# A two-block transformer kernel: the gated linear recurrence reordered, with its decay from an exponential

## The reference

```python
def rg_lru(x, gate_a_w, gate_a_b, gate_x_w, gate_x_b, a_param):
    ...
    r = jax.nn.sigmoid(block_diag(gate_a_w, gate_a_b))
    i = jax.nn.sigmoid(block_diag(gate_x_w, gate_x_b))
    log_a = -LRU_C * r * jax.nn.softplus(-a_param.astype(jnp.float32))
    a = jnp.exp(log_a)
    u = jnp.sqrt(-jnp.expm1(2.0 * log_a)) * (i * x.astype(jnp.float32))
    _, h = lax.associative_scan(linear_combine, (a, u), axis=1)
    return h.astype(x.dtype)

def recurrent_mixer(x, w_in, conv_w, conv_b, gate_a_w, gate_a_b, gate_x_w, gate_x_b, a_param, w_out):
    gate, xr = jnp.split(x @ w_in.astype(x.dtype), [LRU_WIDTH], axis=-1)
    xr = causal_depthwise_conv(xr, conv_w, conv_b)
    h = rg_lru(xr, gate_a_w, gate_a_b, gate_x_w, gate_x_b, a_param)
    return (h * jax.nn.gelu(gate)) @ w_out.astype(x.dtype)
```

## Time and profile before

| what | value |
|---|---|
| time, median of 3 runs | 2933.91 us (2926.31 to 2934.51) |
| the profiled execution's own time | 2934.61 us |
| its span, first to last instruction | 2932.8 us |
| mean granted clock of PE | 0.982 of full speed |
| busy share of the span | PE 96%, DVE 46%, ACT 42%, POOL 42% |
| moved by DMA | 259.21 MB, mean 88 GB/s |
| slabs of weights | 470 in all, 26 made while the recurrence runs |

### The profile page before, as it was taken

One profiled execution on the slowest core, in us unless ns is written; L12 is line 12 of the kernel. 1 busy time (PEld: TensorE's weight loads), 2 busy tenths in 40 slices (PEclk: granted clock), 3 DMA queues, 4 the chain that ended last, 5 costly groups with the idle time before them and its releaser, 6 DMA issues.

```text
span 2932.8 us, 32425 instructions
## 1 busy us (share of the span) xinstructions
PE 2823.6 (96%) x12948; PEld 2281.5 (78%) x12948; DVE 1341.9 (46%) x2091; ACT 1223.7 (42%) x1793; POOL 1236.8 (42%) x550
## 2 busy tenths in 40 slices
PE   8998999999889999998999999999989999999998
PEld 7786788888667888876778788888767777888886
DVE  4565651545875415435656452022246565531113
ACT  3564442434544424334574434233235744342231
POOL 4222344444453444432446444444423464444442
PEclk9999999999989999998999999999999999999999
DMA  4211232232212323322222223232322222223232
GB/s 146 82 59 61 79 101 97 92 107 87 79 65 94 99 91 98 101 92 74 66 65 94 86 94 101 94 100 94 101 72 66 72 79 87 100 94 101 94 101 72
DMA packets 73926, 259.21 MB, mean 88 GB/s; under 512 B 9184, under 2 KB 9184, under 8 KB 73776
## 3 DMA queue, kind: packets, MB, share of 16 engines
q1 hardware_dynamic: 71680, 251.79, 26.8%
q10 hardware_dynamic: 2096, 5.36, 0.5%
HBM read 254.95 MB, written 2.13 MB: 88 GB/s over the span
## 4 chain that ended last, share of the span: by engine, by line
PE 85%; DVE 8%; ACT 3%; issue 2%; POOL 1%; DMA 0%; DVEq 0%; SPq 0%; ACTq 0%; POOLq 0%
PE ps L420 25%; PE ps L422 25%; PE ps L421 25%; PE ps L486 2%; PE ps L516 1%; PE ps L541 1%; PE ps L542 1%; PE ps L543 1%; POOL w_lo L1859 1%; PE ps L499 1%; PE ps L431 1%; PE ps L468 1%; PE ps L470 1%; PE ps L469 1%; ACT w_hi L872 1%
## 5 line engine op out<-in xcount | busy, mean ns | idle before, releaser
L1859 POOL TENSOR_TENSOR w_lo<-raw,w_hi 128x1024 fp32r<-128x1024 f32 x470 | 1135.6, 2419 | 1552.0 <-ACT w_hi L872 1551.6
L420 PE MATMUL ps<-xs,w_hi 128*128 128x512 f32 x2176 | 864.2, 397 | 17.8 <-POOL w_lo L1859 10.3
L421 PE MATMUL ps<-xs,w_hi 128*128 128x512 f32 x2176 | 849.3, 390 | 0.0
L422 PE MATMUL ps<-xs,w_lo 128*128 128x512 f32 x2176 | 849.0, 390 | 0.0
L872 ACT ACTIVATE w_hi<-raw 128x1024 fp32r<-128x1024 f32 x470 | 493.9, 1052 | 660.4 <-PE ps L422 615.4
L420 PE MATMUL ps<-hid,w_hi 128*128 128x512 f32 x1320 | 523.0, 396 | 43.7 <-DVE att L1736 18.1
L421 PE MATMUL ps<-hid,w_hi 128*128 128x512 f32 x1320 | 519.2, 393 | 0.0
L422 PE MATMUL ps<-hid,w_lo 128*128 128x512 f32 x1320 | 519.1, 393 | 0.0
L420 PEld LDWEIGHTS ps<-xs,w_hi 128*128 128x128 f32 x2176 | 409.7, 188 | 123.9 <-issue 15.0
L421 PEld LDWEIGHTS ps<-xs,w_hi 128*128 128x128 f32 x2176 | 410.0, 188 | 88.3 <-issue 4.8
L422 PEld LDWEIGHTS ps<-xs,w_lo 128*128 128x128 f32 x2176 | 409.8, 188 | 86.3
(11 more groups left out here) (212 smaller groups left out, 2651.8 us busy)
## 6 DMA issues: line engine op xcount, KB each, us to landing
raw<-in_weights SPq DMA_DIRECT2D x470, 512.0 KB, 3.5
hT<-in_x ACTq DMA_DIRECT2D x4, 512.0 KB, 9.6
btab<-in_rel SPq DMA_DIRECT2D x8, 256.0 KB, 3.7
out<-tmp ACTq DMA_DIRECT2D x8, 256.0 KB, 2.0
btab<-in_heads SPq DMA_DIRECT2D x6, 256.0 KB, 3.7
tmp<-in_heads SPq DMA_DIRECT2D x6, 256.0 KB, 4.4
common<-in_fixed ACTq DMA_DIRECT2D x1, 642.0 KB, 13.3
small<-in_small ACTq DMA_DIRECT2D x1, 368.5 KB, 5.0
```

Of the source, the lines that this page charges most:

```text
L420: pe.matmul(banks[bank][:], wh, rh, start=(k == 0), stop=False)
L421: pe.matmul(banks[bank][:], wh, rl, start=False, stop=False)
L422: last = pe.matmul(banks[bank][:], wl, rh, start=False, stop=(k == len(specs) - 1))
L1859: gp.tensor_tensor(w_lo[:, n % NPAIR, :], raw[:, n % NRAW, :], w_hi[:, n % NPAIR, :].bitcast(F32), ALU.subtract).then_inc(*w_low.tick(n))
```

## The change

It touches `rec_early` and the stage of the recurrence in each engine's program. The decay a is now an exponential on ACT (L1116 of the changed kernel) of the first tanh; 1-a is then made on DVE as (a+1) times the tangent, and a as one minus that, so the reciprocal goes. The tangent is written to PSUM bank 6 or 7 and the second sigmoid's tanh in place in bank 5, both by ACT, and DVE reads them there. ACT does the exponentials of two tiles and then their square roots together, at c = 3, 5, 7 and 9 (`rec_2`). DVE scans tile c-3, ahead of the taps of tile c, and multiplies the gated input of tile c-1 last. On POOL the product for tile c-3 stands behind the slabs. The banks of `rec_out` are taken in order, its early parts begin at c = 8, and tiles 6 and 7 both are left for the end.

```diff
-        rec_banks = (0, 1, 2, 3, 6, 7, 4, 5)
-        rec_early = {7: [(o, 0, 3) for o in (0, 1, 4, 5)],
-                     8: [(o, 3, 4) for o in (0, 1, 4, 5)] + [(2, 0, 4), (3, 0, 4)],
-                     9: [(o, 4, 6) for o in range(6)], 10: [(o, 6, 7) for o in range(6)]}
+        rec_early = {8: [(o, 0, 4) for o in range(4)], 9: [(4, 0, 4), (5, 0, 4)], 10: [(o, 4, 6) for o in range(6)]}
...
-                    free[bank] = (act, (name, c))
+                free[4], free[5] = (act, ("rec_a", c)), (vec, ("rec_g", c))
...
+            for c in (6, 7):
+                free[c] = (vec, ("rec_w", c))
             for o in range(8):
-                rec_out(o, 7 if o < 6 else 0, 8)
-                free[rec_banks[o]] = (resid, ("rec", o))
+                rec_out(o, 6 if o < 6 else 0, 8)
+                free[o] = (resid, ("rec", o))
...
-                ac.activation(r, r, ACT.Tanh, bias=sp8[:, c:c + 1], scale=sp8[:, c:c + 1]).then_inc(*act.tick(("rec_t", c)))
-                A.wait_ge(act, ("rec_t", c))
-                ac.activation(u, r, ACT.Sqrt).then_inc(*act.tick(("rec_u", c)))
+                if c >= 2:
+                    A.wait_ge(vec, ("rec_w", c - 2))
+                ac.activation(banks[6 + c % 2][:], e, ACT.Tanh, bias=sp8[:, c:c + 1], scale=sp8[:, c:c + 1]).then_inc(
+                    *act.tick(("rec_t", c)))
+
+            def rec_2(tiles):
+
+                for c in tiles:
+                    e = ring(c)[0]
+                    A.wait_ge(act, ("rec_t", c))
+                    ac.activation(e, e, ACT.Exp, bias=s1[:, c:c + 1], scale=s1[:, c:c + 1]).then_inc(*act.tick(("rec_e", c)))
+                for c in tiles:
+                    ac.activation(ring(c)[1], banks[6 + c % 2][:], ACT.Sqrt, scale=0.25).then_inc(*act.tick(("rec_u", c)))
...
             for c in range(12):
+                if c < 8:
+                    weights(("rec_g", c))
+                if c == 0:
+                    root(2)
+                if c in (3, 5, 7, 9):
+                    rec_2((c - 3, c - 2))
                 if 0 <= c - 4 < 8:
                     rec_4(c - 4)
...
-            def rec_2(c):
-                r, gi, u = ring(c)
-                xc, q = att[:, 8 + c, :], tmp[:, 4 + c % 4, :]
-                V.wait_ge(act, ("rec_t", c))
-                if c >= 4:
-                    V.wait_ge(pool, ("rec_y", c - 4))
-                chain(ve.tensor_scalar(q, r, -1.0, -1.0, ALU.mult, ALU.add))
+            def rec_1(c):
                 V.wait_ge(act, ("rec_i", c))
-                ve.scalar_tensor_tensor(out=gi, in0=gi, scalar=1.0, in1=xc, op0=ALU.add, op1=ALU.mult)
+                V.wait_ge(taps, ("rec", c))
+                ve.scalar_tensor_tensor(out=ring(c)[2], in0=banks[5][:], scalar=1.0, in1=att[:, 8 + c, :], op0=ALU.add,
+                                        op1=ALU.mult).then_inc(*vec.tick(("rec_g", c)))
+
+            def rec_3(c):
+
+
+                e, u, gi = ring(c)
+                xc = att[:, 8 + c, :]
+                V.wait_ge(act, ("rec_u", c))
+                chain(ve.scalar_tensor_tensor(out=u, in0=e, scalar=1.0, in1=u, op0=ALU.add, op1=ALU.mult))
+                ve.scalar_tensor_tensor(out=e, in0=e, scalar=1.0, in1=banks[6 + c % 2][:], op0=ALU.add, op1=ALU.mult).then_inc(
+                    *vec.tick(("rec_w", c)))
                 V.wait_ge(step)
-                chain(ve.reciprocal(q, q))
+                V.wait_ge(vec, ("rec_g", c))
+                chain(ve.tensor_tensor(gi, gi, u, ALU.mult))
+                V.wait_ge(vec, ("rec_w", c))
+                chain(ve.tensor_scalar(e, e, -1.0, 1.0, ALU.mult, ALU.add))
                 V.wait_ge(step)
...
+                ve.tensor_tensor_scan(xc, e, gi, 0.0, ALU.mult, ALU.add).then_inc(*vec.tick(("rec_scan", c)))
```

More of the change, by code:

```diff
@@ L1077, in scalar, with rec_gate, rec_in, rec_high @@
             network(0, 1)
[L1080 to L1085 removed]
+            def rec_gate(c):
                 A.wait_ge(scaled, ("rec_g", c))
[L1087 removed]
+                ac.activation(att[:, c, :], banks[2 * (c % 2)][:], ACT.Gelu_apprx_tanh).then_inc(*act.tick(("rec_g", c)))
+            def rec_in(c):
                 A.wait_ge(scaled, ("rec_x", c))
[L1089 removed]
+                ac.activation(att[:, 8 + c, :], banks[2 * (c % 2) + 1][:], ACT.Identity, bias=col("rec_conv_b", c),
                               scale=col("rec_conv_w", 4 * c + 3)).then_inc(*act.tick(("rec_x", c)))
+            def rec_high(c):
                 A.wait_ge(taps, ("rec", c))
@@ L1120, in scalar @@
                 if c < 8:
-                    rec_0(c)
+                    weights(("rec_x", c))
+                    rec_gate(c)
+                if 0 <= c - 1 < 8:
+                    weights(("rec_a", c - 1))
+                    weights(("rec_i", c - 1))
+                if c < 8:
+                    rec_in(c)
                 if 0 <= c - 1 < 8:
                     rec_1(c - 1)
+                if c < 8:
+                    rec_high(c)
                 for o, k0, k1 in rec_early.get(c, ()):
@@ L1563, in rec_0 @@
             def rec_0(c):
-                bg, bx = 2 * (c % 2), 2 * (c % 2) + 1
+                bx = 2 * (c % 2) + 1
                 xc, ps = att[:, 8 + c, :], banks[bx]
-                if c == 0:
-                    root(2)
-                scale(bg, ("rec_g", c), 2, ("rec_g", c))
                 scale(bx, ("rec_x", c), 2, ("rec_x", c))
@@ L1611, in vector @@
             for c in range(12):
+                if c == 0:
+                    root(2)
+                if c < 8:
+                    scale(2 * (c % 2), ("rec_g", c), 2, ("rec_g", c))
                 if 0 <= c - 3 < 8:
                     rec_3(c - 3)
-                if 0 <= c - 2 < 8:
-                    rec_2(c - 2)
                 if c < 8:
                     rec_0(c)
+                if 0 <= c - 1 < 8:
+                    rec_1(c - 1)
             for o in range(8):
-                residual(rec_banks[o], o, ("rec", o), 3, ("rec_out", o))
+                residual(o, o, ("rec", o), 3, ("rec_out", o))
```

45 lines of the change are left out of this document (13 added, 32 removed).

## The result

The changed kernel takes **2925.4 us** (median of 16 runs, 2921.5 to 2928.4) against 2934.1 us (16 runs, 2926.0 to 2935.4) of the kernel before on the same chip. The ratio is 0.9975, 95% interval 0.9967 to 0.9983: some 7.3 us saved (the medians are 8.7 us apart). The sign of the forecast and its range hold; the size does not, since 17.2 us were forecast.

A forecast was written before the change was run, and what follows sets the result against it. The recurrence's loop between DVE and ACT was taken as the bound, PE idling for it. The last operand coming 17.2 us earlier, with the end costing nothing, gave 2934.6 - 17.2 = 2917 us; range 2903 to 2932.

The forecast's parts named there:

- What bounds: In the recurrence, the loop between DVE and ACT sets the pace at 15.26 us per tile, and PE idles for it.
- a floor of 62.0 us for five passes: Recurrence, c = 3 to 7 without meetings with POOL: three odd and two even passes, 41.7 + 20.3 us.
- DVE's wait for the roots at odd c: Sign of being right: in the loop DVE waits 2 to 3 us for ACT's square root at odd c, at even c not.
- I take the middle, 2.6: Recurrence: DVE's meetings with POOL cost 2.6 us per tile, between 2.1 and 3.1; over five passes 13 us.
- then POOL, ACT, POOL 1.26 + 0.63 + 1.26: End of the recurrence: last three terms of the DVE route to the last operand, 26.4 us in all plus 5.2 of meetings.
- costs nothing as long as that chain covers it: Last stretch: PE's 105 matmuls instead of 90, 23.8 + 2.4 us, stay under the 27.3 us chain of DVE and ACT.
- The high part of tile 7 ends near 811 us: Sign of being right: ACT's high part of tile 7 ends at 810.7 us, before at 820.7.
- a last stretch over 27.3: Sign of being wrong: last operand to next root exceeds 27.3 us because PE's 105 matmuls, not the residual chain, fill it.
- Rival (b): Gain eaten, no change: meetings of 3.7 us or more per tile make the end's DVE route count; 2931 us, chance 0.17.
- rival (a): PE becomes the bound: meetings with POOL nearly vanish in the loop, 29.3 us saved, 2905 us; chance 0.17.
- (c): Slower: POOL's every instruction is met in the recurrence, 7 us per tile, 2949 us; chance 0.08.
- (d): Change does not do what it says: ACT or DVE far slower on PSUM in place, loop as before, 2934 us; chance 0.03.

The follow-up runs named there:

- e2: Changed kernel with POOL making only 32 of 1024 columns of each slab's low part in the recurrence; stage 153.9 us against the changed kernel's 177.0.
- e4: Changed kernel with POOL's product of tile c-3 moved behind the gate's slab, ahead of the low part and the input's slab; stage 163.5 us, ratio 0.9941.
- e6: Changed kernel with POOL's late slabs of c = 10 issued with those of c = 11, behind tile 7's low part; stage 172.6 us, ratio 0.9952.
- e11: Changed kernel with tile 6's product made early at c = 11, one tile left for the end; stage 174.2 us, ratio 0.9964.
- e10: Kernel before with only the new table of the early output product and banks in plain order; stage 178.7 us, ratio 0.9978.
- e5: Changed kernel with POOL's whole order from the kernel before: low part, product, then slabs; stage 174.5 us, ratio 0.9966.
- e9: Kernel before with only POOL's order altered: gate's slab, product, low part, input's slab; stage 184.4 us, ratio 1.0000.
- e3: Changed kernel with 1-a written in place in PSUM, so the TENSOR_SCALAR reads PSUM; stage 172.9 us, ratio 0.9961.
- e8: Changed kernel with exponential and root made for one tile in every pass instead of batches of two; stage 175.8 us, ratio 0.9960.

## Why the prediction was right in sign and wrong in size

- **What bounds** was right: the loop between DVE and ACT, until tile 7, and then the way to the last operand. So was the recurrence's own path: a floor of 62.0 us for five passes against 64.5 in e2; table loads at 1.28 us; PSUM operands never met, at 0.68 us instead of the 0.75 assumed; DVE's wait for the roots at odd c, 2.8, 3.8 and 3.8 us instead of 2 to 3.
- **The first failed step is "I take the middle, 2.6".** The five passes, from 731.78 to 811.05, took 79.3 us, so (79.3 - 62.0) / 5 = 3.5 us per tile in place of 2.6: 4.3 of the 4.5 us missing in the loop. (It is what the passes take above the path without meetings; the four groups by themselves lose 3.0 us per tile, as a mean of all eight.) Even the upper bound of 3.1 was too low. It took the meetings as a rate that goes with the number of exposed instructions. They go with the place: the changed kernel's run of five begins when POOL has been given its low part and slabs, and the product that could have held POOL back stands behind them. One call moved (e4) brings the excess of the four groups from 3.0 to 0.8 us per tile, or 1.2 with the input's low part on DVE, which is now met instead.
- **The second is the route of DVE at the end**, "then POOL, ACT, POOL 1.26 + 0.63 + 1.26". The order of POOL above shows two slabs between these two instructions of POOL; they were not in the sum. From the product's start to the last operand it took 7.2 us instead of 3.2. The other terms held: PE until the slab 8.6 against 9.2, the batch 4.7 against 4.8, the two scans with their meetings 11.6 against 12.7. The middle is 2.8 us longer than the forecast's, and e6, without the slabs in between, gives it back.
- **The third is "costs nothing as long as that chain covers it"** for the 15 matmuls moved behind the last operand. 23.8 + 2.4 us of matmuls were set against a chain of 27.3, as if they ran side by side; but the chain starts only when PE has closed the first block, and the slabs for the later blocks stand in it on ACT and, as a meeting, on DVE. The last stretch took 29.5; with tile 6 early (e11) 26.5. From the first block's sum to the root, 1.7 of the 2.4 us come with the table (e10), as an instruction of DVE of 0.75 us that takes 2.3 to 2.4 beside a slab. Of the other 0.7, 0.4 lie between the first and the second sum: PE, behind its wait of 5.0 us, gives its matmuls 0.43 us apart there (granted clock 0.53 from 845 to 850) and closes the second block late. The chain stayed the bound, and it got longer itself.
- **The shares were wrong too.** The forecast gave 10 us to the recurrence and 7.2 to the table. The recurrence gave 5.5; the table by itself gives 5.7 in the stage (e10). On top of the table the rest of the change brings only 178.7 - 177.0 = 1.7 us, since of the 5.5 of its loop 3.7 are lost in its end (64.1 against 60.4), the slabs ahead of the low part among it.
- "The high part of tile 7 ends near 811 us" looks right in the trace (811.05 + 0.63) and is not: this execution came 3.6 us early into the stage. Places in a trace are to be compared from a common row.
- **The signs.** POOL's waits for ACT were to fall and rose, from 58.4 to 68.7 us. The first product to the root took 182.6 us instead of 173. Of the signs of being wrong one came: a last stretch over 27.3, which is 29.7 in the forecast's rows (845.70 to 875.39), though by the longer chain and not by PE.
- Rival (b)'s mechanism, meetings above the forecast's bounds, is the nearest, but its condition of 3.7 us per tile is not reached at 3.5, and the time lies between the forecast's 2923 and its 2931. The small-slab run e2 shows rival (a)'s loop: PE has no wait in it until 790.4 us, and the loop is 20.3 us shorter than before, against 22.1 worked out. That its whole stage is 30.5 us shorter, against 29.3, is in part luck, for the small slabs also shorten the end. (c) and (d) have nothing for them.

## What to carry over

When two engines get in each other's way, the price is not a rate per instruction: lay the two queues side by side and see which instruction of the one stands beside which of the other. An engine that has to wait anyway should wait in front of the neighbour's exposed run, with one urgent piece of its work ahead of the wait (e4), not behind it (e5). That this pays has to be tried: the same order gave the kernel before nothing (e9). And time each independent part of a change by itself: here a new table for the early product gave by itself three quarters of what the whole change gives.

## What was unexpected of the hardware

- A TENSOR_SCALAR of 128x512 on DVE, 0.40 us alone, took 2.05 us on average in the changed kernel (2.5 us in the chain above), 0.44 in e2, and 0.68 when it reads PSUM (e3): slower than alone, but 0.68 is also its mean over all eight tiles.
- The load of a table on ACT costs 1.28 us with nothing around it, also when there are 22 in a stage of 175.8 us (e8).
- Half of a wait moved to the next exposed instruction: in e3 the TENSOR_SCALAR lost 1.38 us and the scan behind it gained 0.66.
